# Reordering the end of each expert in a two-block transformer kernel: down projection by output halves, transposes ahead of the gathers

## What is computed

```python
def swiglu(h, w_gate, w_up, w_down):
    return (jax.nn.silu(h @ w_gate) * (h @ w_up)) @ w_down

def moe_swiglu(h, w_router, w_gate, w_up, w_down):
    logits = (h @ w_router).astype(jnp.float32)
    top_val, top_idx = lax.top_k(logits, TOP_K)
    top_w = jax.nn.softmax(top_val, axis=-1)
    gates = jnp.sum(jax.nn.one_hot(top_idx, N_EXPERTS, dtype=jnp.float32) * top_w[..., None], axis=-2)
    out = jnp.zeros_like(h)
    for e in range(N_EXPERTS):
        y = swiglu(h, w_gate[e], w_up[e], w_down[e])
        out = out + gates[..., e:e + 1].astype(h.dtype) * y
    return out
```

## Time and profile before

| | us |
|---|---|
| median of three runs | 1962.61 |
| span of the profiled execution, first to last instruction | 1958.3 |
| median less this span | 4.3 |
| TensorE busy in the span | 1850.7 (95%) |
| VectorE busy | 1397.2 (71%) |
| ScalarE busy | 1149.9 (59%) |
| GpSimd busy | 1004.6 (51%) |

### The profile page before, as it was taken

How to read it: one execution, slowest core, us unless ns; L and a number is a source line. 1 busy time by engine, 2 the same in 40 slices (tenths; PEclk the granted TensorE clock), 3 DMA queues, 4 the chain that set the end, 5 groups by cost and what they waited for, 6 DMA issues and landing times.

```text
span 1958.3 us, 27080 instructions
## 1 busy us (share of the span) xinstructions
PE 1850.7 (95%) x9874; PEld 1579.4 (81%) x9874; DVE 1397.2 (71%) x1164; ACT 1149.9 (59%) x955; POOL 1004.6 (51%) x488
## 2 busy tenths in 40 slices
PE   6978999998899999999999999999999899889999
PEld 5868999887787887887877878878788697779998
DVE  5755445645678887888787888878888766367775
ACT  4534444465476676776766767767677454535553
POOL 6430000000596885977968869779597314620000
PEclk9988999999899999999999999999999898679999
DMA  7334555451699897998988989989899433215551
GB/s 235 103 118 133 194 194 194 151 172 65 228 377 348 327 369 273 374 365 308 373 319 323 371 303 378 363 309 370 306 376 365 154 115 108 86 44 172 179 187 65
DMA packets 248534, 479.51 MB, mean 245 GB/s; under 512 B 15919, under 2 KB 84297, under 8 KB 248409
## 3 DMA queue, kind: packets, MB, share of 16 engines
q1 hardware_dynamic: 247545, 476.49, 68.4%
q10 hardware_dynamic: 864, 1.31, 0.2%
HBM read 476.72 MB, written 1.05 MB: 244 GB/s over the span
## 4 chain that ended last, share of the span: by engine, by line
PE 82%; DVE 8%; issue 5%; ACT 3%; POOL 1%; DVEq 0%; DMA 0%; SPq 0%; ACTq 0%; POOLq 0%
PE bank L1823 24%; PE bank L1825 24%; PE bank L1824 24%; DVE wl L1436 3%; PE bank L2094 2%; PE bank L2171 2%; ACT wh L993 1%; PE bank L2124 1%; PE bank L1908 1%; PE bank L1789 1%; DVE arena L1474 1%; PE bank L2232 0%; DVE xT L1219 0%; DVE arena L1545 0%; DVE arena L1469 0%
## 5 line engine op out<-in xcount | busy, mean ns | idle before, releaser
L1823 PE MATMUL bank<-wh,xTh 128*128 128x512 f32 x1584 | 631.8, 399 | 24.1 <-DVE xTl L1519 8.3
L1825 PE MATMUL bank<-wh,xTl 128*128 128x512 f32 x1584 | 620.7, 392 | 0.0
L1824 PE MATMUL bank<-wl,xTh 128*128 128x512 f32 x1584 | 620.2, 392 | 0.0
L795 POOL TENSOR_TENSOR wl<-raw,wh 128x512 fp32r<-128x512 f32 x224 | 540.1, 2427 | 128.4 <-ACT wh L993 112.0
L1436 DVE TENSOR_TENSOR wl<-raw,wh 128x1536 fp32r<-128x1536 f32 x224 | 489.7, 2205 | 78.2 <-ACT wh L993 76.6
L993 ACT ACTIVATE wh<-raw 128x2048 fp32r<-128x2048 f32 x224 | 429.0, 1917 | 139.0 <-PE bank L1825 139.0
L1823 PEld LDWEIGHTS bank<-wh,xTh 128*128 128x128 f32 x1584 | 299.9, 189 | 91.4 <-DVE wl L1436 18.8
L1825 PEld LDWEIGHTS bank<-wh,xTl 128*128 128x128 f32 x1584 | 299.3, 189 | 64.1
L1824 PEld LDWEIGHTS bank<-wl,xTh 128*128 128x128 f32 x1584 | 300.1, 189 | 61.1 <-issue 1.4
L795 POOL TENSOR_TENSOR wl<-arena,wh 128x512 fp32r<-128x512 f32 x112 | 301.9, 2709 | 73.0 <-ACT wh L993 73.0
L438 DVE TENSOR_TENSOR wl<-raw,wh 128x2048 fp32r<-128x2048 f32 x110 | 257.8, 2360 | 73.7 <-ACT wh L431 72.0
(11 more groups left out here) (352 smaller groups left out, 1672.4 us busy)
## 6 DMA issues: line engine op xcount, KB each, us to landing
raw<-in_moe_w_up SPq DMA_DIRECT2D x112, 1024.0 KB, 5.3
arena<-in_moe_w_gate SPq DMA_DIRECT2D x96, 1024.0 KB, 5.3
raw<-in_moe_w_down SPq DMA_DIRECT2D x96, 1024.0 KB, 5.4
raw<-in_w_up SPq DMA_DIRECT2D x22, 1024.0 KB, 5.2
raw<-in_moe_w_gate SPq DMA_DIRECT2D x16, 1024.0 KB, 5.2
arena<-in_moe_w_down SPq DMA_DIRECT2D x16, 1024.0 KB, 5.8
raw<-in_gla_w_in SPq DMA_DIRECT2D x12, 1024.0 KB, 5.6
raw<-in_w_in SPq DMA_DIRECT2D x12, 1024.0 KB, 5.1
```

The source lines that it names most:

```text
L795: V.tensor_tensor(wl[:, s, LO_V:PIECE], moe_raw(c)[0][:, LO_V:PIECE], wh[:, s, LO_V:PIECE].bitcast(F32), ALU.subtract).then_inc(lo_moe[1], 1)
L1823: T.matmul(o, xh, yh, start=first, stop=False)
L1824: T.matmul(o, xh, yl, start=False, stop=False)
L1825: return T.matmul(o, xl, yh, start=False, stop=last)
```

## The change

TensorE: `transposed(6)` moves from between the two gathers to between the two pieces of `down(5)` (the argument `between`). Both gathers follow `down(5)` without a break. `down(6)` becomes `last_down`: it goes through both pieces for output half 0, signals `moe_y0full`, and goes through both pieces again for half 1; the pieces are given back by `moe_used` only in the second turn. The scatters of half 0 wait for `ey`'s first half and use banks 7 and 4, those of half 1 wait for the second half and use banks 5 and 6; none waits for an addition any more.

ScalarE: `actT_hi(6)` comes one step earlier, ahead of the rounding of the next expert's first piece, and the copy of `bank[5]` comes one step earlier and waits for `moe_y0full`. VectorE: `actT_lo(6)` and the low part of the next expert's second piece come ahead of both `gather_out`; the additions go in the order (t, half) = (0,0), (1,0), (0,1), (1,1).

The core of the diff:

```diff
@@ -1033,10 +1033,10 @@
                         tail = (kind, j, k) == ("d", NEJ - 2, 1)
-                        if tail:
+                        if (kind, j, k) == ("d", NEJ - 2, 0):
                             actT_hi(NEJ - 1)
-                        if (kind, j, k) == ("d", NEJ - 1, 1):
-                            act.wait_ge(sg("moe_used"), at(PC, UC * (i + 1)))
+                        if (kind, j, k) == ("d", NEJ - 1, 0):
+                            act.wait_ge(sg("moe_y0full"), at(2, i + 1))
                             V.activation(ey[:, 0:512], bank[5][:, :], ACT.Copy).then_inc(sg("moe_y0"), 1)
@@ -1054,7 +1054,7 @@
             for t in range(TT):
-                act.wait_ge(sg("moe_h"), more * 8 + (8 * NPAIR + 1 - 2 * (TT - 1 - t)))
+                act.wait_ge(sg("moe_h"), more * 8 + (8 * NPAIR + 1 - (TT - 1 - t)))
                 A(V.activation(junk, h[:, t, :], ACT.Square, accum_out=ssq[:, 2 * t:2 * t + 1]), "ssq_ready")
@@ -1526,10 +1526,11 @@
                         if tail:
+                            actT_lo(NEJ - 1)
+                        weights_lo(q)
+                        if tail:
                             gather_out(0, bank[7], at(4, 2 * i + 3))
-                            actT_lo(NEJ - 1)
                             gather_out(1, bank[(NEJ * (i + 1)) % 2], at(4, 2 * i + 4))
-                        weights_lo(q)
                         if not more_follow and UC * i + q + NW >= PC:
@@ -1552,10 +1553,10 @@
                     for q in range(4):
-                        t, half = q // 2, q % 2
+                        t, half = q % 2, q // 2
                         dve.wait_ge(sg("moe_scfull"), at(8, 4 * i + q + 1))
                         hs = h[:, t, half * 512:(half + 1) * 512]
-                        V.tensor_tensor(hs, hs, bank[7 if q % 2 == 0 else 4][:, :], ALU.add).then_inc(sg("moe_h"), 1)
+                        V.tensor_tensor(hs, hs, bank[(7, 4, 5, 6)[q]][:, :], ALU.add).then_inc(sg("moe_h"), 1)
                     weights_lo(UC - 2)
@@ -1564,7 +1565,7 @@
             for t in range(TT):
-                dve.wait_ge(sg("moe_h"), more * 8 + (8 * NPAIR + 1 - 2 * (TT - 1 - t)))
+                dve.wait_ge(sg("moe_h"), more * 8 + (8 * NPAIR + 1 - (TT - 1 - t)))
                 C(V.tensor_tensor(xn[:, t, :], h[:, t, :], fgain, ALU.mult), "hg")
@@ -2124,18 +2125,41 @@
-                    def down(j):
+                    def down(j, between=None):
                         n = NEJ * i + j
...
                         for part in range(2):
+                            if part and between is not None:
+                                between()
                             h_, l_ = here(UC * i + upos["d", j, part], 2)
...
                                     ins = mm3(bank[5 + half][:, :], eactTh[:, kk, :], eactTl[:, kk, :], h_[:, k, hs], l_[:, k, hs],
-                                              j == 0 and part == 0 and k == 0, j == NEJ - 1 and part == 1 and k == 1)
+                                              j == 0 and part == 0 and k == 0, False)
                             used(ins)
+
+                    def last_down():
+
+                        n = NEJ * i + NEJ - 1
+                        pe.wait_ge(sg("moe_actTl"), at(2 * NEJ, n + 1))
+                        for half in range(2):
+                            hs = slice(half * 512, (half + 1) * 512)
+                            for part in range(2):
+                                h_, l_ = here(UC * i + upos["d", NEJ - 1, part], 2)
+                                for k in range(2):
+                                    kk = 4 * (n % 2) + 2 * part + k
+                                    ins = mm3(bank[5 + half][:, :], eactTh[:, kk, :], eactTl[:, kk, :], h_[:, k, hs], l_[:, k, hs],
+                                              False, part == 1 and k == 1)
+                                if half:
+                                    used(ins)
+                            if half == 0:
+                                ins.then_inc(sg("moe_y0full"), 1)
+
+                    def scatter(t, half, b):
+                        T.matmul(b[:, :], ohT[:, t * P:(t + 1) * P], ey[:, half * 512:(half + 1) * 512],
+                                 start=True, stop=True).then_inc(sg("moe_scfull"), 1)
@@ -2147,7 +2171,9 @@
                         gate_up(bank[2 + n % 2], "u", j)
-                        if j:
+                        if j == NEJ - 1:
+                            down(j - 1, lambda: transposed(NEJ - 1))
+                        elif j:
                             down(j - 1)
@@ -2158,18 +2184,15 @@
                     gather(0, bank[7])
-                    transposed(NEJ - 1)
                     gather(1, bank[(NEJ * (i + 1)) % 2])
-                    down(NEJ - 1)
+                    last_down()
+                    pe.wait_ge(sg("moe_xg"), at(4, 2 * i + 4))
                     pe.wait_ge(sg("moe_y0"), at(2, i + 1))
+                    scatter(0, 0, bank[7])
+                    scatter(1, 0, bank[4])
                     pe.wait_ge(sg("moe_y1"), at(2, i + 1))
-                    pe.wait_ge(sg("moe_xg"), at(4, 2 * i + 4))
-                    for q in range(4):
-                        t, half = q // 2, q % 2
-                        if q >= 2:
-                            pe.wait_ge(sg("moe_h"), at(8, 4 * i + q))
-                        T.matmul(bank[7 if q % 2 == 0 else 4][:, :], ohT[:, t * P:(t + 1) * P],
-                                 ey[:, half * 512:(half + 1) * 512], start=True, stop=True).then_inc(sg("moe_scfull"), 1)
+                    scatter(0, 1, bank[5])
+                    scatter(1, 1, bank[6])
```

## The result

The changed kernel takes 1976.22 us (median of four runs, 1970.79 to 1977.90), beside 1963.03 us for the kernel before: a ratio of 1.006, with a 95% interval of 1.0043 to 1.0076. It is slower, by 13 us in the medians. The forecast was slower by 6.2 us, 1968.8 us in a range of 1965.8 to 1972.5. So the sign came out, and the size is twice the forecast and outside the range.

A forecast was written before the change was run, and what follows sets the result against it. TensorE, busy 95% of the span, was taken as the bound. Each of eight experts loses 2.11 us and saves 1.33 at the scatter, net 0.78; 6.2 us more makes 1968.8 us, range 1965.8 to 1972.5.

The forecast's parts named there:

- The transposes' wait: At each expert's end, TensorE stands still 2.04 us before block 6's transposes, until VectorE's multiplication of block 6 ends.
- the transposes among weight matmuls: The four transposes inside `down(5)` cost 0.51 us, against 0.44 between the gathers, adding 0.07 us per expert.
- the scatter: From the end of `last_down` to the next expert's first matmul: about 3.53 us instead of 4.86, saving 1.33 per expert.
- rival B: GpSimd's part goes before VectorE's low part, so TensorE waits 0.25 us at `last_down`: 1970.8 us in all; chance 0.09.
- A: Rival: the multiplication is not late; without any wait each expert saves 1.26 us, 1952.5 us in all; chance 0.12.
- C: Rival: scatters of half 1 wait for VectorE's copy, so the 1.33 us saving is lost: 1979.5 us; chance 0.04.
- The same matmuls in another order: Step for TensorE behind the wait: gathers keep 3.62 us, `last_down` 5.45, transposes add 0.07; its end comes 2.11 us later.
- T: The moment `last_down` ends on TensorE at an expert's end; forecast 2.11 us later than before.
- rival D: The loop-restart pause behind experts two and four, if fixed in end, absorbs 0.78 us twice: 1967.3; inside the forecast's 0.75.

## Why the prediction was wrong

Right: the sign, and the place. The transposes' wait is 2.04 us at each expert, forecast 2.04, released by the multiplication. Right within a few hundredths: the transposes among weight matmuls (0.49, forecast 0.51), the scatter (3.45, forecast 3.53). No wait opened at `last_down`: `actT_lo` was done at 630.25, and TensorE came there at 633.1 (at 631.5 had the clock held). So rival B did not happen. At this place VectorE and GpSimd work on the two parts of the same piece:

```profile
627.88 1.76 DVE L1436 TENSOR_TENSOR wl<-raw,wh 128x1536 fp32r<-128x1536 f32 x1 [3.18 <-ACT wh L993]
627.93 2.85 POOL L795 TENSOR_TENSOR wl<-raw,wh 128x512 fp32r<-128x512 f32 x1 [2.69 <-ACT wh L993]
```

B had the order wrong. VectorE started first and took about its shortest time (1.75), and GpSimd ended 1.14 us after VectorE's end, where its own work takes 1.27 alone. The lock that B took from the Trainium skill's page "SBUF — State Buffer", section "SBUF: two separate sides", agrees with this to 0.13 us: by that page whichever starts first has the ports for its whole instruction. But `actT_lo` stands behind VectorE's part, which did not wait. A and C did not happen either.

Wrong, the step that failed: in "The same matmuls in another order" I took every matmul behind the wait at the 0.227 us of the rows before, that is, at a granted clock of 1.00, and so put T 2.11 us later. Behind the wait the clock was 0.5 for a stretch, and eight matmuls went at 0.43: another 1.57 us at each of eight experts, 12.6 us in this profile. Both kept profiles of this kernel have it at all eight; how many experts have it in its faster runs is not known. The rows of before had a pause of 2.78 us at the restart with a clock of 1.00 behind it, which I read silently as leave to ignore a wait of 2.04; no rival named the clock. Filling the wait shows that this is the cause.

A second, smaller miss: rival D and the forecast took the restart's pause as it was, or as soaking up a delay. It became shorter by 1.0 and 1.6 us here, for a reason that stays open, and that luck hides 2.6 us of the first miss.

The half of the change that I priced as a gain is one: alone it gives 7 us, and with the multiplication moved the whole change gives 10.

## What to carry to other kernels

Before a consumer on the bound engine is moved forward, follow its producer's queue and not only its operation: here a multiplication of 0.7 us was done 4.7 us after its inputs, as a low part stood ahead of it, and moving that producer turned a loss of 10 us and more into a gain of 10. A wait on TensorE costs its length and may cost the clock of a stretch behind it; price both, and give the second a range, since the same wait took the clock down at eight of eight experts in one kernel and at two of eight in another. Where a wait can't be avoided, work that serves nothing in it can be cheaper than idleness.

## What the runs showed of the hardware that was not expected

**A wait of 2 us can halve the clock.** In the changed kernel 2.04 us without matmuls brought a stretch of about 3.4 us at 0.5 at all eight experts, in two profiles on two occasions; with the same wait in the kernel with the transposes alone it came at two of eight; with 1.36 us of it left (one `mm3` in the gap) the profile showed it at none of the eight. The length of the pause alone does not decide: at the loop's restart 2.78 and 2.94 us left the clock at 1.00 in the kernel before, while 2.83 us with the scatter's half alone and 2.52 us in the version with the one-hot steps moved had a stretch at 0.5 behind them. What decides between such cases stays open.

**The pause at a loop's restart varies.** Ahead of the first matmul of a new pass, TensorE stood idle for 2.8 and 2.9 us in the kernel before, 1.8 and 1.4 in the changed one, 5.0 and 2.8 in the one with the scatter's half alone. Beside the pause of before stands a transfer of two packets on the queue of instructions:

```profile
q8 instruction: 2, 0.03, 1.6%
```

so it may be the wait for instructions to be loaded. That was only argued, no run tested it: the same two packets stand beside the shorter pause of the changed kernel (1.76 us), and what sets its length stays open. The two pauses together came to between 3.1 and 7.9 us in the kernels told here, against 5.7 before, and for that reason differences of some 2 us are not told as gains.
